# VectorE and ScalarE each run their steps in an order of their own, by work behind each step, with a reach of four

## What is computed

```
for i in range(2):                       # block 0: "fox" mixer, block 1: "mla" mixer
    h = rmsnorm(x, norm_mix[i])
    p = h @ w_in                         # queries, keys, values, memory queries
    o = concat(attention(p), memory_cross(p, k_mem, v_mem))
    x = x + o @ w_out[i]
    x = x + conv_ffn(rmsnorm(x, norm_ffn[i]))     # up 1024 -> 2 x 2816, conv of 3, silu * value, down
...                                      # third block: half of a gated FFN, then
                                         # window attention + convolution of 31 taps (a GLU before it,
                                         # a layer norm and silu behind it) + memory, w_out_2,
                                         # then half of a second gated FFN
```

## Time and profile before

| | |
|---|---|
| median of 3 runs | 2168.46 us (2167.44 to 2168.91) |
| the profiled execution's own time | 2170.62 us |
| its span (first to last instruction) | 2168.8 us |
| TensorE busy (matmuls) | 2101.9 us, 97% |
| TensorE busy (weight loads) | 1746.2 us, 81% |
| VectorE busy | 1269.0 us, 59% |
| ScalarE busy | 938.4 us, 43% |
| mean granted TensorE clock | 0.991 |

### The profile page before, as it was taken

How to read it: one execution, slowest core, us unless ns; L and a number is a source line. 1 busy time by engine, 2 the same in 40 slices (tenths; PEclk the granted TensorE clock), 3 DMA queues, 4 the chain that set the end, 5 groups by cost and what they waited for, 6 DMA issues and landing times. The chain is left out here.

```text
span 2168.8 us, 30188 instructions
## 1 busy us (share of the span) xinstructions
PE 2101.9 (97%) x11177; PEld 1746.2 (81%) x11177; DVE 1269.0 (59%) x2131; ACT 938.4 (43%) x1898; POOL 49.1 (2%) x95
## 2 busy tenths in 40 slices
PE   7999999999999898999999999999999889999999
PEld 7899778788888776788888888888888667888887
DVE  7655567737755675776477544344448856443442
ACT  7655444424435764543244333223344554322331
POOL 0000001000001110000000000000001000000000
PEclk9999999999999998999999999999999999999999
DMA  6212123332332011233333333333332112333332
GB/s 214 79 59 59 58 74 98 103 101 89 97 102 89 15 35 31 77 100 105 94 97 96 103 97 98 97 94 99 93 95 64 30 45 87 98 101 94 97 97 93
DMA packets 101667, 187.33 MB, mean 86 GB/s; under 512 B 11408, under 2 KB 12048, under 8 KB 101264
## 3 DMA queue, kind: packets, MB, share of 16 engines
q1 hardware_dynamic: 101520, 185.39, 27.6%
HBM read 183.25 MB, written 2.10 MB: 85 GB/s over the span
## 5 line engine op out<-in xcount | busy, mean ns | idle before, releaser
L1808 DVE TENSOR_TENSOR WL<-RAW,WH 128x512 fp32r<-128x512 f32 x681 | 458.2, 689 | 356.1 <-ACT WH L2075 334.4
L1628 PE MATMUL PSA<-HNh,WH 128*128 128x512 f32 x1440 | 563.7, 391 | 5.8 <-DVE HNl L1797 4.6
L1629 PE MATMUL PSA<-HNl,WH 128*128 128x512 f32 x1440 | 560.3, 389 | 0.0
L1630 PE MATMUL PSA<-HNh,WL 128*128 128x512 f32 x1440 | 560.3, 389 | 0.0
L2075 ACT ACTIVATE WH<-RAW 128x512 fp32r<-128x512 f32 x681 | 413.1, 625 | 313.3 <-PE PSA L1630 221.3
L1628 PEld LDWEIGHTS PSA<-HNh,WH 128*128 128x128 f32 x1440 | 270.3, 188 | 67.0 <-DVE HNl L1797 7.9
L1629 PEld LDWEIGHTS PSA<-HNl,WH 128*128 128x128 f32 x1440 | 270.4, 188 | 56.8 <-issue 1.2
L1630 PEld LDWEIGHTS PSA<-HNh,WL 128*128 128x128 f32 x1440 | 270.3, 188 | 56.4
L1628 PE MATMUL PSA<-Gh,WH 128*128 128x512 f32 x704 | 274.1, 389 | 2.0 <-DVE Gl L1970 2.0
L1629 PE MATMUL PSA<-Gl,WH 128*128 128x512 f32 x704 | 273.9, 389 | 0.0
L1630 PE MATMUL PSA<-Gh,WL 128*128 128x512 f32 x704 | 273.9, 389 | 0.0
(11 more groups left out here) (254 smaller groups left out, 2448.8 us busy)
## 6 DMA issues: line engine op xcount, KB each, us to landing
RAW<-in_w SPq DMA_DIRECT2D x681, 256.0 KB, 2.6
XT<-in_x SPq DMA_DIRECT2D x8, 256.0 KB, 5.2
MT<-in_mem SPq DMA_DIRECT2D x2, 1024.0 KB, 6.5
out_x<-XT SPq DMA_DIRECT2D x8, 256.0 KB, 2.0
PAR<-in_par SPq DMA_DIRECT2D x1, 207.0 KB, 6.9
CB<-in_cb SPq DMA_DIRECT2D x1, 96.0 KB, 6.8
PAR<-in_par SPq DMA_DIRECT2D x1, 84.5 KB, 2.0
PT<-in_const SPq DMA_DIRECT2D x1, 70.0 KB, 5.4
```

The source lines that it names most:

```text
L1628: pe.matmul(out, wh, xh, start=(a["start"] and c == 0), stop=False)
L1629: pe.matmul(out, wh, xl, start=False, stop=False)
L1630: p = pe.matmul(out, wl, xh, start=False, stop=ends)
L1808: dve.tensor_tensor(l[:, :], r[:, :], h[:, :], ALU.subtract).then_inc(done.sem("split.dve"), 1)
```

## The change

The three programs of TensorE, GpSimd and SyncE keep the list's order. VectorE and ScalarE get an order of their own. At build time, every engine's program is run once against a recorder (`Trial`), which notes each share's waits, signals and an assumed length. `Arranged` then plays all five programs against these lengths. When VectorE or ScalarE comes free, it looks at the first four shares that it has left, and takes the one that can begin first; among those that can begin at once, the one with the longest chain of work behind it over all engines (`far`). Shares of one kind keep their order among themselves, and so do the sections between ScalarE's table loads. The order so found is written into the program; nothing is decided on the chip. Two entries of the list are taken apart, so that the engine may do other work in between: `gate` into three, and `gated` into `gsilu`, `gmul` and `gated`. No computation, buffer or transfer is added or removed.

```diff
+class Arranged:
...
+            for i, p in enumerate(t.parts):
+                for c in chains(e, p) if e in free else [0]:
+                    if c in prev:
+                        j = prev[c]
+                        self.due[self.first[e, i]].append((self.first[e, j] + len(t.parts[j].phases) - 1, -1.0))
+                    prev[c] = i
...
+        for x in reversed(order):
+            self.far[x] = self.took(x) + LANDING[self.node[x][0]] + max((self.far[y] for y in self.after[x]), default=0.0)
...
+                reach = self.reach if e in self.free else 1
+                found = None
+                for i in todo[e][:reach]:
+                    t = open_at(self.first[e, i])
+                    if t is None or blocked(e, i):
+                        continue
+                    t = max(t, clock[e])
+                    z = (t, -self.far[self.first[e, i]], e, self.first[e, i], i)
+                    if found is None or z[:2] < found[:2]:
+                        found = z
...
-                    step("gated", key, conv=conv, g=g, bank=b, q=q,
+                    if conv:
+                        step("gsilu", key)
+                    step("gmul", key, conv=conv, g=g, bank=b)
+                    step("gated", key, q=q,
...
-            for s in steps:
+            for s in turns(act, "act"):
...
+        def chains(e, p):
+            return [("kind", p.kind)]
+
+        arranged.append(Arranged(trials, ("dve", "act"), 4, chains))
```

More of the change, by code:

```diff
@@ L151, with __init__, does, waits_for @@
         ("pscore", (1, 0, 0)): 5, ("pscore", (1, 0, 1)): 10, ("pturn", (1, 0, 0, 0)): 14, ("pscore", (2, 0, 0)): 12}
+class Part:
+    def __init__(self, kind, key, step):
+        self.kind, self.key, self.step, self.phases = kind, key, step, [([], [])]
+        self.time, self.section = [0.0], None
+    def does(self):
+        return self.time[-1] > 0 or self.phases[0] != ([], [])
+    def waits_for(self, sem, value):
+        if self.time[-1]:
+            self.phases.append(([], []))
+            self.time.append(0.0)
+        self.phases[-1][0].append((sem, value))
+    def takes(self, t):
+        self.time[-1] += t
+    def raises(self, sem, n):
+        self.phases[-1][1].append((sem, n, self.time[-1]))
@@ new lines, with __init__, took, rank @@
+LANDING = {"pe": 0.23, "dve": 0.17, "act": 0.19, "pool": 0.2, "sp": 3.0}
+class Arranged:
+    def __init__(self, trials, free, reach, chains):
+        self.trials, self.free, self.reach = trials, free, reach
+        raised = {}
+        self.first, self.node = {}, []
+        for e, t in trials.items():
+            t.parts = t.parts[:1] + [p for p in t.parts[1:] if p.does()]
+            for i, p in enumerate(t.parts):
+                self.first[e, i] = len(self.node)
+                for f in range(len(p.phases)):
+                    self.node.append((e, i, f))
+        self.level = {}
+        for x, (e, i, f) in enumerate(self.node):
+            for sem, n, t in trials[e].parts[i].phases[f][1]:
+                self.level[sem] = self.level.get(sem, 0) + n
+                raised.setdefault(sem, []).append((self.level[sem], x, t))
+        self.after = [[] for _ in self.node]
+        self.due = [[] for _ in self.node]
+        for x, (e, i, f) in enumerate(self.node):
+            if f:
+                self.due[x].append((x - 1, None))
+            for sem, value in trials[e].parts[i].phases[f][0]:
+                y = next(z for z in raised[sem] if z[0] >= value)
+                if y[1] != x:
+                    self.due[x].append((y[1], y[2]))
+        for e, t in trials.items():
+            prev = {}
+            for i, p in enumerate(t.parts):
+                for c in chains(e, p) if e in free else [0]:
[3 more added lines that the diff above has]
+                    prev[c] = i
+            if e in free:
+                behind, now = [], []
+                for i, p in enumerate(t.parts):
+                    if p.section is None:
+                        continue
+                    if now and t.parts[now[-1]].section != p.section:
+                        behind, now = now, []
+                    self.due[self.first[e, i]] += [(self.first[e, j] + len(t.parts[j].phases) - 1, -1.0) for j in behind]
+                    now.append(i)
+        for x, d in enumerate(self.due):
+            for y, t in d:
+                self.after[y].append(x)
+        self.rank()
+        self.order = {e: [] for e in trials}
+        self.run()
+    def took(self, x):
+        e, i, f = self.node[x]
+        return self.trials[e].parts[i].time[f]
+    def rank(self):
+        left = [len(d) for d in self.due]
+        order, open_ = [], [x for x, n in enumerate(left) if not n]
+        while open_:
+            x = open_.pop()
+            order.append(x)
+            for y in self.after[x]:
+                left[y] -= 1
+                if not left[y]:
+                    open_.append(y)
+        assert len(order) == len(self.node)
+        self.far = [0.0] * len(self.node)
+        for x in reversed(order):
+            self.far[x] = self.took(x) + LANDING[self.node[x][0]] + max((self.far[y] for y in self.after[x]), default=0.0)
+    def run(self):
+        end, begun = [None] * len(self.node), [0.0] * len(self.node)
+        engines = list(self.trials)
+        clock = {e: 0.0 for e in engines}
+        todo = {e: list(range(len(self.trials[e].parts))) for e in engines}
+        at = {e: None for e in engines}
+        def open_at(x):
+            t = 0.0
+            for y, lag in self.due[x]:
+                if end[y] is None:
+                    return None
+                same = self.node[y][0] == self.node[x][0]
+                if lag is None or lag < 0:
+                    t = max(t, end[y])
+                else:
+                    t = max(t, begun[y] + lag + LANDING[self.node[y][0]])
+            return t
+        def blocked(e, i):
+            x = self.first[e, i]
+            return any(end[y] is None and self.node[y][0] == e and self.node[y][1] != i
+                       for z in range(x, x + len(self.trials[e].parts[i].phases)) for y, lag in self.due[z])
+        while any(todo.values()) or any(x is not None for x in at.values()):
+            best = None
+            for e in engines:
+                if at[e] is not None:
+                    t = open_at(at[e])
+                    if t is not None:
+                        t = max(t, clock[e])
+                        if best is None or t < best[0]:
+                            best = (t, 0.0, e, at[e], None)
+                    continue
+                reach = self.reach if e in self.free else 1
[3 more added lines that the diff above has]
+                    if t is None or blocked(e, i):
+                        continue
+                    t = max(t, clock[e])
+                    z = (t, -self.far[self.first[e, i]], e, self.first[e, i], i)
+                    if found is None or z[:2] < found[:2]:
+                        found = z
+                if found and (best is None or found[0] < best[0]):
+                    best = found
+            assert best, "nothing can begin"
+            t, _, e, x, i = best
+            if i is not None:
+                todo[e].remove(i)
+                self.order[e].append(i)
+            begun[x], end[x] = t, t + self.took(x)
+            clock[e] = end[x]
+            part = self.trials[e].parts[self.node[x][1]]
+            at[e] = x + 1 if self.node[x][2] + 1 < len(part.phases) else None
+        self.end = max(clock.values())
+    def steps(self, e):
+        return [self.trials[e].parts[i].step for i in self.order[e][1:]]
@@ L1233, in gates @@
         def gates(g):
-            step("gate", 0, g=g, banks=[PS[t][:, 256:268] for t in range(4)], total=("totalc.act", "mix0"))
+            step("gatein", 0, g=g, banks=[PS[t][:, 256:268] for t in range(4)], total=("totalc.act", "mix0"))
+            step("gate", 0)
+            step("gatelow", 0)
             def cum():
@@ L1798, in stt @@
                 return ins
-            for s in steps:
+            for s in turns(dve, "dve"):
                 k, key, a = s.kind, s.key, s.a
@@ L2264, in turned @@
                 return pool.tensor_tensor(out, M[0], M[1], ALU.add)
[L2266 removed]
+            for s in turns(pool, "pool"):
                 k, key, a = s.kind, s.key, s.a
@@ L2329, in sync @@
             sp.dma_start(POSI[:, :, :], io["pos"]).then_inc(s_pos, 16)
-            for s in steps:
+            for s in turns(sp, "sp"):
                 k, key, a = s.kind, s.key, s.a
```

116 lines of the change are left out of this document (101 added, 15 removed).

## The result

The changed kernel takes 2111.12 us (median of 4 runs, 2110.87 to 2114.49) against 2168.52 us for the kernel before (4 runs, 2167.44 to 2168.91). The ratio is 0.974, with a 95% interval of 0.9723 to 0.9757. The profiled execution took 2110.87 us.

What follows compares the result with a forecast made beforehand. TensorE was taken to bound the kernel, with a matmul under way 2101.9 of 2168.8 us. Waits removed 18.0 plus clock 8.6 minus 8.9 given back make 17.7 us less: 2168.5 to 2150.8 us, 8-in-10 range 2133 to 2168.

Steps and rivals of the forecast that it cites:

- all three places: Late exponentials near 706 and 1708 and low part near 825: TensorE waits for engines that had other work ready.
- Mostly given back: Rival: waits move to the next step of the same chain, clock still falls; 6.7 us stays, 2161.8 us; chance 0.12.
- buffers: Rival: waits for bank 6 and evacuations only move with the PSUM bank's chain; 14.2 us gain, 2154.3 us; chance 0.05.
- no effect: Rival: TensorE waits on latency chains that no order shortens; within 4.3 us of before; chance 0.09.
- slower: Rival: assumed lengths put attention's splits and copies behind waiting shares, some 5 us per new wait; with five, 2174; chance 0.09.
- all of it: Rival: waits are pure queueing, half-clock stretches go with them, nothing new appears; 2133.3 us; chance 0.15.
- the six kinds of wait in the earlier trace: TensorE's waits for exponentials, low part, evacuations, splits, bank 6's multiply and copies; 16.5 us predicted to go.
- The rest: Small TensorE waits at the FFN's splits and at low parts behind taps; 1.5 us predicted to go.
- clock: Six TensorE stretches at half clock, 37.4 us, each following a wait, lose 17.2 us; half, 8.6, predicted regained.
- given back: Next waits, uncovered waits and ordering faults return a third of 26.6 us: 8.9 us.
- low part: Turned queries' low part near 825, queued behind maxima, exponentials and a split; its 2.3 us wait goes whole.
- Some 60 us can answer: Claimed ceiling: of the 2168.8 us, some 60 can in principle answer to this change, and no more.

Runs made afterwards that it cites:

- reach of two: Changed kernel with VectorE and ScalarE looking at two shares instead of four when choosing the next; 2115.24 us, ratio 0.9758.
- run with 34 warm matmuls: Kernel before, list order on all engines, with 34 instead of 14 warm matmuls ahead of the 3.54 us wait at 706; 2167.52 us, ratio 0.9996.
- run with one wait put back: Changed kernel with four more serial 128x512 ScalarE activations, results unused, ahead of the second block's first exponentials; 2112.76 us, ratio 0.9746.

## Why the prediction was wrong

The mechanism was right: queueing behind waiting shares, read from three timelines, and all three places did as described. *Mostly given back*, *buffers*, *no effect* and *slower* are out by the time alone, and even *all of it* was 22 us too slow. The sizes were wrong, by 59.7 − 17.7 = 42.0 us of span:

| term | predicted | measured | off by |
|---|---|---|---|
| the six kinds of wait in the earlier trace rows | 16.5 | 31.2 − 9.2 = 22.0 | 5.5 |
| **"The rest", all other waits** | 1.5 | 20.5 | 19.0 |
| clock | 8.6 | 13.8 | 5.2 |
| given back | −8.9 | −7.9 | 1.0 |
| first load, later by chance | 0 | −0.7 | −0.7 |
| busy time around waits | not in the sum | 12.0 | 12.0 |

*The step that failed is "The rest".* Of 66.9 us of idle time 6.7 are the first load, 3.2 lie behind the last matmul, and 31.2 are the six kinds that I listed. 25.8 us were left, in 40 listed waits, the longest 1.7 us, and some too short for the list: some 11 us in 690 to 900, 8 in the third mixer and 5 in 60 to 690, where I had said that all would stay as before. I gave them 1.5 without following one of them back. They now sum to 33.0 − 7.4 − 3.2 − 9.2 = 13.2, of which 7.9 are new or grown: the sum RS (2.8), copies PT (1.8), YK (2.1 more), PT of VectorE (1.2 more). So 25.8 − (13.2 − 7.9) = 20.5 us went. Gone are the waits of wide matmuls for low parts (4.6 us, seven times), for residual sums (2.8) and for Gl (2.0). One of them followed back has the same cause as the long ones. Before:

```profile
295.20 0.68 DVE L1808 TENSOR_TENSOR WL<-RAW,WH 128x512 fp32r<-128x512 f32 x1
295.81 0.68 DVE L1947 TENSOR_TENSOR XT<-PSA,XT 128x512 f32<-128x512 f32 x1
...
298.08 0.50 PE L1628 MATMUL PSA<-HNh,WH 128*128 128x512 f32 x1 [1.08 <-DVE HNl L1797]
```

A split stands ahead of the residual sum XT, from which HNh and HNl follow. In the changed kernel the sum begins at 290.02, the split behind it at 291.22, and the wait is gone. The others I have not followed one by one; that the order removed them is shown, since the run with the list's order has nearly all of them still.

*Six kinds.* Exponentials 7.2 us (taken: 6.0), low part 2.3 (2.3), evacuation 3.0 (1.7), splits 2.5 (3.0), multiply 4.2 (2.0), copies 2.8 (1.5). The halvings and thirds that I chose within their bounds were mostly too careful: with a reach of two already, 52.5 of the 57 us came. The splits' 2.5 us are no firm number: the trace of before has two waits for them in the first 20 us, that of the run with 34 warm matmuls, with the same order there, has three, of 0.84, 1.45 and 1.40 us. At 706 the wait is 1.16 us, not under 1. In a small thing the recorded working was loose as well: the exponentials of the earlier trace rows were ready for 1.6 us of the 2.89 that ScalarE stood still, since their maxima ended at 703.15.

*Clock.* Of the six stretches five are gone, and the one at 1709 is left at half its length (1666.9 now). I took half for want of a row. The run with one wait put back shows the row: a wait of 3.67 us brought the half clock back, where the changed kernel's waits of 1.80 and 1.61 us, at 702 and 710, had none behind them. The length of a single wait does not settle it, though: the stretch at 1666.9 comes with waits of 0.49 and 1.08 us. And of the 13.8 us some 2 may be the scatter between executions.

*Given back.* The size was about right (7.9 of idle time, 8.9 taken), but it was to be a third of a sum that was twice too small, so that it came out near is luck. The 2.8 us of RS come with 3.4 us at half clock and ate the start's gain, so the squares and splits there brought nothing net. The first load's 0.7 us are no effect of the order: TensorE's first matmul began between 6.5 and 7.8 us in the experiments too.

*The ceiling.* "Some 60 us can answer" is the idle time of the two attention stretches and the clock's 17.2, and left out the rest of the rows: 57.0 us of idle time without the first load and the 3.2 behind the last matmul, plus 17.2, are 74, and most waits cost 0.16 us each beyond that.

*The other engines' terms.* That ScalarE's and VectorE's orders are one gain was in the working (the head norm, the exponentials), but not that VectorE alone would bring 45 us. That gain is not in the long waits for exponentials, of which VectorE's order alone left 2.97 of 3.54 and all 1.50 us, but in the low part's wait, the five for bank 6 (5.5 us, none listed any more), the copies (3.3 us, now 1.0), and, out of "The rest", in the waits of wide matmuls for low parts, residual sums and Gl, of which none is listed with VectorE's order alone.

*Queues and buffers.* The Trainium skill (PSUM — Partial Sum Buffer, Engine vs sequencer instructions) says that the queues of ScalarE, VectorE and GpSimd are strictly first in, first out. The 2.89 us of ScalarE idle ahead of exponentials that were ready for the last 1.6 of them agree, and so does the gain from order alone. The Trainium skill (Perfetto Trace Analysis, Optimization Strategy) says that a gap that repeats on the busy engine can mean too few buffers in SBUF or PSUM. The waits for bank 6 fell from 5.5 to 1.3 us with not one buffer more, so here the measurement speaks against that reading.

## What to carry to other kernels

Where engines run a fixed program, let each pass one blocked share before looking for anything finer: here reach two without new buffers brought 2.4%, and a longer reach or a priority moved it by a few us, to either side. When costing such a change, sum *all* idle time of the bounding engine by cause, the small waits too, and add what each wait costs around it: half clock behind the long ones, and the overlap of matmuls that is lost at each. A single wait changed can be taken up by the next ones, as the run with one wait put back shows; the many shortened together here were not. To learn which engine's queue holds a wait, free one engine at a time and look at that wait, not at the total. After the change, look again at fillers that were tuned for the old waits, and at the program's start, where choosing by the longest chain can put off what the bounding engine needs first.

## What the hardware showed that I had not expected

TensorE's busy time fell by 25.8 us with the same matmuls. At one place the half clock could be switched both ways: on by a delay of ScalarE's that made a wait of 3.67 us, off by 34 idle matmuls of 0.17 us in a kernel that had 14. And one delay of 2.5 us cost 0.3 us of idle time but 2.3 us of clock. VectorE's instruction on 128x16 elements took 0.16 us in one kernel and 1.25 us in the other, where an instruction of GpSimd's was under way, and stood ahead of maxima that TensorE waited for. The stretches at half clock also move from one execution to the next where the order of work is the same.
